# Query-key dots of a two-layer attention step: from two 64-row float32 matmuls to float32r halves on all 128 rows

## The reference, cut to what matters

```python
q_a, k_a, v_a, gate_a, q_i, k_i, w_i, q_b, k_b, v_b, gate_b = split_cols(h @ w_in)
q_a, k_a, q_i, k_i = rope(...)                         # 8, 2, 4 and 1 heads of dim 64
rel   = relu(einsum('bqhd,bsd->bqhs', q_i, k_i))       # index dots: 4 heads, one shared key
score = einsum('bqhs,bqh->bqs', rel, w_i) * IDX_SCALE  # masked to the chunk limit
_, idx = top_k(score, topk)                            # 256 keys of a query, 80 for the sample
logits = einsum('bqngd,bqknd->bqngk', q_a, k_a[idx]) * HD_A ** -0.5
o_a = softmax(logits) @ v_a[idx]
o_b = group_norm(retention(q_b, k_b, v_b, s0))
x = x + gate * rms_norm(concat(o_a * silu(gate_a), o_b * silu(gate_b)) @ w_out)
```

## Time and profile before

| | us |
|---|---|
| median of 3 executions | 1431.36 (1430.39 to 1431.76) |
| the profiled execution | 1430.55 |
| its span on the core | 1428.7 |
| TensorE matmuls, busy | 1380.3 |
| VectorE, busy | 1010.9 |
| ScalarE, busy | 783.7 |
| GpSimd, busy | 405.2 |

### The profile page before, as it was taken

One profiled execution on the slowest core, in us unless ns is written; L12 is line 12 of the kernel. 1 busy time (PEld: TensorE's weight loads), 2 busy tenths in 40 slices (PEclk: granted clock), 3 DMA queues, 4 the chain that ended last, 5 costly groups with the idle time before them and its releaser, 6 DMA issues.

```text
span 1428.7 us, 24483 instructions
## 1 busy us (share of the span) xinstructions
PE 1380.3 (97%) x7623; PEld 1054.7 (74%) x7623; DVE 1010.9 (71%) x2991; ACT 783.7 (55%) x1916; POOL 405.2 (28%) x382
## 2 busy tenths in 40 slices
PE   6999999999999999999988999999999999999997
PEld 2865777788887677668877587877888766766786
DVE  0787899999996555542398789999999754554225
ACT  2555666666326665664454566666632566666432
POOL 3741332444421011001387123443343100100110
PEclk9999999999999999999999999999999999999999
DMA  9743333211232112223252111211223211221325
GB/s 317 230 133 106 96 121 115 78 29 54 58 92 66 42 39 69 82 65 106 93 186 62 40 32 51 52 43 40 62 58 88 68 32 46 71 66 61 116 78 175
DMA packets 125191, 122.05 MB, mean 85 GB/s; under 512 B 33256, under 2 KB 94024, under 8 KB 125064
## 3 DMA queue, kind: packets, MB, share of 16 engines
q1 hardware_dynamic: 124608, 120.36, 28.1%
q10 hardware_dynamic: 456, 0.13, 0.0%
HBM read 93.55 MB, written 26.90 MB: 84 GB/s over the span
## 4 chain that ended last, share of the span: by engine, by line
PE 55%; DVE 33%; issue 5%; POOL 2%; DMA 2%; ACT 1%; DVEq 0%; ACTq 0%; SPq 0%; POOLq 0%
DVE U L1782 12%; PE proj L1017 10%; PE proj L1018 9%; PE turn L996 9%; PE proj L1020 9%; PE logit L1044 7%; PE out_bank L1071 5%; PE spare L1044 2%; DVE turned L1737 2%; DVE by_cos_sin L1722 2%; DVE by_cos_sin L1720 2%; DVE probsT_more L1855 2%; DVE probsT_more L1859 1%; POOL h_lo L1560 1%; DVE U L1876 1%
## 5 line engine op out<-in xcount | busy, mean ns | idle before, releaser
L1017 PE MATMUL proj<-w_hi,h_hi 128*128 128x512 f32 (+2 forms) x1440 | 574.4, 399 | 3.0 <-POOL h_lo L1560 2.2
L1018 PE MATMUL proj<-w_lo,h_hi 128*128 128x512 f32 (+2 forms) x1440 | 535.3, 372 | 0.0
L1020 PE MATMUL proj<-w_hi,h_lo 128*128 128x512 f32 (+2 forms) x1280 | 477.4, 373 | 0.0
L1554 POOL TENSOR_TENSOR w_lo<-w_raw,w_hi 128x512 fp32r<-128x512 f32 (+2 forms) x160 | 202.9, 1269 | 741.5 <-ACT w_hi L1260 741.3
L1017 PEld LDWEIGHTS proj<-w_hi,h_hi 128*128 128x128 f32 x1440 | 271.9, 189 | 53.3 <-issue 15.8
L1018 PEld LDWEIGHTS proj<-w_lo,h_hi 128*128 128x128 f32 x1440 | 272.1, 189 | 31.0
L1020 PEld LDWEIGHTS proj<-w_hi,h_lo 128*128 128x128 f32 x1280 | 240.2, 188 | 37.1
L1782 DVE TENSOR_SCALAR_CACHE_REDUCE U<-score,cand 128x384 bf16<-128x384 f32 x310 | 223.0, 752 | 2.4 <-DVE cand L1799 0.3
L1044 PE MATMUL logit<-keys,queries 64*128 64x512 f32 (+4 forms) x454 | 137.2, 542 | 2.3 <-ACT U L1403 1.6
L1383 ACT ACTIVATE probsT_more<-turn 128x512 f32<-128x512 f32 (+3 forms) x156 | 76.1, 491 | 96.0 <-PE turn L996 95.8
L996 PEld LDWEIGHTS turn<-ident,U 128*128 128x128 f32 x604 | 68.4, 140 | 52.7 <-issue 36.9
(11 more groups left out here) (203 smaller groups left out, 2109.0 us busy)
## 6 DMA issues: line engine op xcount, KB each, us to landing
w_raw<-in_w_in_dram SPq DMA_DIRECT2D x80, 256.0 KB, 3.3
probsT_more<-in_w_ada_dram SPq DMA_DIRECT2D x64, 256.0 KB, 3.9
score<-mixed_dram SPq DMA_DIRECT2D x36, 256.0 KB, 3.0
score<-in_w_ada_dram SPq DMA_DIRECT2D x32, 256.0 KB, 5.1
w_raw<-in_w_out_dram SPq DMA_DIRECT2D x32, 256.0 KB, 3.4
U<-in_x_prompt_dram SPq DMA_DIRECT2D x12, 512.0 KB, 4.1
mixed_dram<-U SPq DMA_DIRECT2D x24, 192.0 KB, 2.1
gates_dram<-U SPq DMA_DIRECT2D x18, 256.0 KB, 2.1
```

The lines of the kernel that those rows point to most:

```text
L1017: nc.tensor.matmul(out, h_hi[:, k, tile], hi, start=(k == 0), stop=False)
L1018: ins = nc.tensor.matmul(out, h_hi[:, k, tile], lo, start=False, stop=(t == SAMPLE and k == KT - 1))
L1020: ins = nc.tensor.matmul(out, h_lo[:, k, tile], hi, start=False, stop=(k == KT - 1))
L1554: nc.gpsimd.tensor_tensor(w_lo[:, s % WS, 0:w], w_raw[:, n % RAWS, 0:w], w_hi[:, s % WS, 0:w].bitcast(F32), ALU.subtract).then_inc(w_lo_re ...
```

## The change

- `queries` is float32r and holds each head on all 128 partitions: one half has the high half of the head, the other the low half (high is the value rounded to float32r, low the rest). `keys` becomes `keys_hi` and `keys_lo`, with the same 64 rows on both halves of the partitions. A dot is now two float32r matmuls on 128 rows into one bank, against `keys_hi` and against `keys_lo`.
- ScalarE copies the whole turned operand (384 columns) raw into `raw_turn`, which is the scratch tile `by_cos_sin`. It waits for that copy and writes the high halves of the queries in two copies of 64 partitions.
- VectorE makes the low halves of the queries (`lower_queries`, two subtractions on 64 partitions): in `idx` steps in q = 2 ahead of `weigh_relus`, in `att` steps behind all quarters.
- GpSimd rounds the keys and makes their low part (`split_keys`, `split_cache`), behind its other work of the step.
- `rope` and the sample's low-row copy use the same scratch tile, so both wait until both splits are done. TensorE's dots wait for both splits too, where they waited for ScalarE's copy.
- To make room, the weight rings have 14 slices. Slices 6 and 7 of each chunk, which were prepared at the start of the steps that project tiles 6 and 7, are prepared together in q = 1 of the step that projects the sample tile, once TensorE has done the first quarter of that tile.

```diff
+def late_slices(g):
+    return [weight_slice(g - n) for n in range(LATE, 0, -1)] \
+        if 0 <= g < STEPS and g % NT == SAMPLE and g // NT + 1 < DEPTH * NCH else []
...
-WS = 2 * KT
+WS = 2 * KT - 2
+LATE = 2 * KT - WS
...
-        keys = sb("keys", [P, NKEYS])
-        queries = sb("queries", [P, 2, GROUP // 2, P])
+        keys_hi = sb("keys_hi", [P, NKEYS], F32R)
+        keys_lo = sb("keys_lo", [P, NKEYS], F32R)
+        queries = sb("queries", [P, 2, GROUP, P], F32R)
...
+        raw_turn = by_cos_sin[:, 0:384]
...
-                    rows_ = slice(HD * (h % 2), HD * (h % 2) + HD)
                     key = ("l", g, h, p)
-                    ring.filled(nc.tensor.matmul(ring.bank(key)[:, 0:m], queries[rows_, HILO[g] % 2, h // 2, :],
-                                                   keys[rows_, k0 + a:k0 + a + m], start=True, stop=True), key)
+                    out, both_halves = ring.bank(key)[:, 0:m], queries[:, HILO[g] % 2, h, :]
+                    nc.tensor.matmul(out, both_halves, keys_hi[:, k0 + a:k0 + a + m], start=True, stop=False)
+                    ring.filled(nc.tensor.matmul(out, both_halves, keys_lo[:, k0 + a:k0 + a + m],
+                                                 start=False, stop=True), key)
...
-                    turns_of(g).wait_taken(pe, ("q", g))
+                    pe.wait_ge(queries_split, HILO[g] + 1)
+                    pe.wait_ge(keys_split, HILO[g] + 1)
...
-                nc.scalar.activation(queries[:, HILO[g] % 2], src[:, 0:256].rearrange("p (h n) -> p h n", n=P), ACT.Copy)
-                ring.take(nc.scalar.activation(keys[:, blk * P:(blk + 1) * P], src[:, 256:384], ACT.Copy), ("q", g))
+                ring.take(nc.scalar.activation(raw_turn, src[:, 0:384], ACT.Copy), ("q", g))
+                ring.wait_taken(act, ("q", g))
                 wait_keys_free(act, g)
+                for half in (0, 1):
+                    at = slice(HD * half, HD * half + HD)
+                    ins = nc.scalar.activation(queries[at, n % 2, half::2, :],
+                                               raw_turn[at, 0:256].rearrange("p (h n) -> p h n", n=P), ACT.Copy)
+                ins.then_inc(queries_high, 1)
...
+                    if q == 1:
+                        for s in late_slices(i + 1):
+                            split_weights(s)
...
+                for s in late_slices(i + 1):
+                    lower_weights(s)
                 for l, t in hidden_turns(i - 1):
                     if l == 0 and i >= 0:
                         lower_hidden(l, t)
+                if kind(i) in ("idx", "att"):
+                    split_keys(i)
...
+                if splits_before(g):
+                    dve.wait_ge(queries_split, splits_before(g))
+                    dve.wait_ge(keys_split, splits_before(g))
...
+            def lower_queries(g):
+                n = HILO[g]
+                dve.wait_ge(queries_high, n + 1)
+                for half in (0, 1):
+                    have, other = (slice(HD * h, HD * h + HD) for h in (half, 1 - half))
+                    ins = nc.vector.tensor_tensor(queries[other, n % 2, half::2, :],
+                                                  raw_turn[have, 0:256].rearrange("p (h n) -> p h n", n=P),
+                                                  queries[have, n % 2, half::2, :].bitcast(F32), ALU.subtract)
...
+                    if q == TURN_QUARTER and kind(i) == "idx":
+                        lower_queries(i)
...
+                if kind(i) == "att":
+                    lower_queries(i)
                 if mixed_turn(i):
                     lower_mixed(*mixed_turn(i))
```

82 lines of the change are left out of this document (64 added, 18 removed).

## The result

| | before | after |
|---|---|---|
| median, us | 1430.93 (4 executions) | 1457.78 (4 executions) |
| ratio, 95% interval | | 1.0186 (1.0169 to 1.0202) |
| span of the profiled execution, us | 1428.7 | 1455.2 |

What follows compares the result with a forecast made beforehand. TensorE's time was taken to count in full in attention, with the index stages closer to a loop through all engines. Net terms 4.2 - 1.4 + 0.6 gave 3.4 us gained, a median of 1428, range 1418 to 1438.

Steps and rivals of the forecast that it cites:

- TensorE: Cheaper dots and no changes of kind: a gain of 12.3 us in attention, 6.0 in each index stage, 24.3 in all.
- attention: Both layers' attention: TensorE's gain of 12.3 us less costs of 8.1, a net gain of 4.2 us.
- The group of 512 keys: Two heads' dots against 512 keys: 1.06 us before; new formula m/600 and 0.06 us for m keys.
- change of kind: Between a projection and a float32 dot on TensorE: each costs 0.1 us, and should go with float32r.
- (a): Last three steps of `ATT1`: the subtractions stand ahead of `lower_mixed`, which frees the banks; cost 6 x 0.75 = 4.5 us.
- (b): Tile 7 in attention: ScalarE also gets the two late slices; cost 2.4 us for both layers (bounds 0 and 8).
- (c): Tiles 1 to 3 in attention: a margin near 0 for the hand-over; cost 12 x 0.1 = 1.2 us.
- Cost in idx, layer 1: Index stage of layer 1: a loop of 8.4 us against 7.9; six steps at 0.9, cost 5.4, net gain 0.6 us.
- Cost in idx, layer 0: Index stage of layer 0: rope waits for `split_keys` (3.8 us), longer hand-over (3.6); cost 7.4 against a gain of 6.0.
- four steps near 0.9: Index stage of layer 0, from tile 3 on: longer hand-over ahead of h_hi and h_lo against faster dots; cost 3.6 us.
- Elsewhere: Late slices in `ret`, `gate` and `out`, needed some 9 us on: counted as nothing, at most 2 us.
- The loop decides: Rival: hand-over through three engines takes 0.6 us more than counted in each of 14 index steps; 1436 us, chance 0.24.

Runs made afterwards that it cites:

- e4: The changed kernel, but index steps hand the turned operand over as before, with the low halves left out: 1419.68 us.
- e3: The kernel before with only the weight rings of 14 slices and the late slices: 1435.35 us, ratio 1.0025.
- e5_att_late: The changed kernel, but in attention VectorE makes the queries' low halves at the end of its step, behind `lower_mixed` and the sample's selection chain: 1456.85 us.
- e6: The changed kernel with the sums of q = 2 ahead of the subtractions in index steps and the raw copy in its own slots: 1440.12 us.
- e7: The changed kernel with the raw copy in its own slots and, in index steps, without VectorE's two subtractions (queries' low halves left out): 1426.99 us.
- e12: The exact version splitting from the bank (1432.3), with the subtractions ahead of the sums in one index step, t = 4 of layer 1: 1432.77 us.
- e13: The exact version splitting from the bank (1432.3), with the subtractions ahead of the sums of q = 2 in step t = 3 of layer 1: 1431.52 us.
- e2: The changed kernel, but the raw copy goes to free slots of the ring for projected rows, so rope no longer waits for both splits: 1452.75 us.
- e1: The changed kernel, but in index steps VectorE makes the queries' low halves behind the weighted sums of q = 2: 1447.98 us.
- e9: The changed kernel with six extra products of 512 columns on TensorE in two places of layer 0 where it stood still: 1457.33 us.
- e8_from_bank: The changed kernel, but in index steps ScalarE and VectorE split straight from the bank, GpSimd does nothing; attention subtractions at the step's end: 1432.32 us.
- e10_gpsimd_low: The changed kernel with the raw copy in its own slots and, in index steps, GpSimd making the queries' low halves instead of VectorE: 1461.09 us.

## Why the prediction was wrong

**Right for the group, too low in attention: TensorE.** The group of 512 keys (0.92 forecast, 0.93 measured), that of 128 keys (0.48; the starts from 450.99 to 451.49 give 0.50), no cost for a change of kind. The gain in the index parts was 9.3 instead of 12.0 (e4 against e3). In attention it was larger than the 12.3 forecast, which is 0.12 us a group: eight steps of layer 0 in which TensorE waits neither before nor after (the fifth to seventh of `ATT0`, the third to seventh of `ATT1`) are 4.5 us shorter with 20 groups, 0.23 each. The change of kind was counted at the start of the dots and at a projection behind them; in the sixth step of `ATT0` the first two turns behind them are 0.16 us apart before and 0.11 now as well. The Trainium skill's "TensorE: Matmul & The Clock Gate" (Part 3: Packing small matmuls) gives as the cure for few rows to run several matmuls at once, and I had concluded from it that heads which already run side by side leave nothing to gain. The runs show a gain: e4_old_handover is 15.7 us below e3_late_slices.

**Right in sum, by luck: attention.** A gain of 4.2 was forecast and 6.5 came. At 0.23 us a group TensorE gains some 23 us in 104 groups (an estimate), where I had 12.3; the costs are then near 17, where I had 8.1. Two terms, each off by about a factor of two, cancel. (a) `lower_mixed`: TensorE's waits for it are 2.9 us in six cases, not 4.5, and e5_att_late, which takes the subtractions out of its way, gets 1.6 back in those steps. (b) The late slices: e3 puts 1.3 us on the two layers, not 2.4. (c) "Tiles 1 to 3 have a margin near 0", 1.2 us: the third step of `ATT0` alone pays 3.4 us in layer 0 and 4.2 in layer 1. There the selection chain stands in VectorE's queue, which I had not looked for.

**Wrong: "Cost in idx, layer 1", 5.4 us.** The new hand-over costs 15.2 there (e4 to after). I wrote down a loop of one rope, six sums, one hand-over, 8.4 us against 7.94. That is 0.5 more, and the 0.9 a step that I charged does not follow from it. The loop left out the scaling of the next inputs (1.36 us an operation group, up to twice a step), which the index steps of layer 1 also have in their first tiles. By e6 and e7 VectorE's two subtractions cost 11.9 us there even behind the sums, and by e12 and e13 moving one step's subtractions only moves the wait. The term asks what one step's loop takes; the rows fit better with VectorE's total work in the chunk, which grew by 7.7 us (e4 to e13).

**Wrong: "Cost in idx, layer 0", 7.4 us.** This is the term that failed most: it is 22.7 (e4 to after). I followed one wait, `rope` behind `split_keys` behind h_lo, and priced it at 3.8; the shared tile is worth 1.3 there alone (e2), 3.4 with the sums first (e1 to e6), and 5.0 in the whole kernel (e2). I had not followed two others. TensorE's dots wait for `keys_lo` directly, five times 1.1 us: of the 8.3 us of e7 that is the larger part. And `lower_queries` holds the sums back by up to 2.9 us, into the time of h_lo: 9.2 us (e2 to e6). I had named that order in the change and for layer 1, and then had counted for layer 0 only the longer hand-over, "four steps near 0.9". The wait delayed all that VectorE had queued behind it, and this term was not in the sum at all.

**Wrong: "Elsewhere", "I count nothing, at most 2 us".** The weight rings cost 4.0 us. "Needed three quarters into the next step, some 9 us on" took an average step; the sample's steps of `ret`, `gate` and `out` are 3.6 to 6.6 us long.

**Missing: the clock.** Seven low stretches belong to no term. I had read 1.00 in the rows of before and kept it. Where the cost of one can be read it is 1.6 us (e9). No run removed them, so what they cost in sum stays open, below 12 us.

**Rivals.** "The loop decides" (1436, 0.24) had the right sign and engines, with 0.6 us a step; from the third step on those of layer 0 pay 1.3 to 7.2 us, and those of layer 1 from -0.7 to 2.3, with 3.8 in the step behind them. The point of decision, 3.7 us between turn and split, was judged from ScalarE's and VectorE's durations alone. In the step shown above the query halves were done 3.0 us behind the turn, so the hand-over I had costed was right, and yet the step lost 7 us. What decided was the queue behind the wait. The stretching that I had set inside a term of 0.9 us does show: two sums took 1.64 and 1.57 instead of 0.75 beside GpSimd's h_lo. The Trainium skill's "SBUF — State Buffer" (Who interferes with whom) has a VectorE instruction with two SBUF inputs contend with a GpSimd instruction that reads SBUF, and these rows agree in direction. It does not decide by its own length: over the index chunks, VectorE's time above the shortest row of each line and form is 14.2 us against 11.7 before in layer 0, and 11.4 against 8.2 in layer 1.

**Open.** The runs were not made to tell how much of the 9.2 us of order in layer 0 is the stretching beside h_lo. No version of the change here beats the kernel before; e8_from_bank and e13_by_step_t3 equal it. With 1419.7 us for the old hand-over, which leaves the low halves out, the room is at most 11 us. To take the low halves off VectorE is not enough for it: on GpSimd they cost more (e10_gpsimd_low).

## What to carry to other kernels

When a change adds a wait to an in-order queue, price what is queued behind that wait on its engine until the first row that another engine waits for. In layer 0 the duration of the new operations was the smaller part; in layer 1, where VectorE was busy for 86% of the index chunk without them, the chunk grew by about their duration (8.2 us for 7.7, e4 to e13). Ask of each new product on an engine at the end of a chain who now waits for it directly: GpSimd's extra load was free, the wait for its result was not. And a new wait of TensorE can cost twice, since the clock was low for a while behind seven of the thirteen long ones here.

## What was not expected of the hardware

- The granted clock fell to 1.2 GHz behind an idle stretch of TensorE of 1.54 us (0.50 in 85.50:88.40). With the stretch filled by 1.56 us of products it stayed at 1.00. It did not fall behind every one: the wait of 3.1 us near 140 us has 1.00 behind it in the changed kernel and 0.50 in e9_filler, and 1.6 us of time lie between the two.
- GpSimd needs 0.73 us for a subtraction of 64x256 where VectorE needs 0.42 (e10_gpsimd_low, L1641; L1828), and VectorE's own goes up to 1.4 beside GpSimd.
